# Building the gate one-hots of a PEER layer token by token, with keys in a row, in place of four wide comparisons and products a batch

## The reference

```
v1, i1 = top_k(s1, 16);  v2, i2 = top_k(s2, 16)            # per token and head (8 heads)
vals, ci = top_k(v1[:, None] + v2[None, :], 16)
e = i1[ci // 16] * 128 + i2[ci % 16]                       # 128 picks a token
g = softmax(vals)
a = gelu(x . u_tab[e])
out = sum_k g[k] * a[k] * v_tab[e[k]]
```

## Time and profile before

| what | us |
|---|---|
| three runs | 2448.03, 2458.07, 2462.87 (median 2458.07) |
| profiled execution | 2466.9 |
| its span | 2465.1 |
| TensorE busy | 2270.6 (92%) |
| VectorE busy | 1850.8 (75%) |
| ScalarE busy | 1188.8 (48%) |
| GpSimd busy | 422.4 (17%) |

### The profile page before, as it was taken

One profiled execution on the slowest core, in us unless ns is written; L12 is line 12 of the kernel. 1 busy time (PEld: TensorE's weight loads), 2 busy tenths in 40 slices (PEclk: granted clock), 3 DMA queues, 4 the chain that ended last, 5 costly groups with the idle time before them and its releaser, 6 DMA issues. The chain is left out here.

```text
span 2465.1 us, 33782 instructions
## 1 busy us (share of the span) xinstructions
PE 2270.6 (92%) x11984; PEld 1244.1 (50%) x11984; DVE 1850.8 (75%) x4125; ACT 1188.8 (48%) x1631; POOL 422.4 (17%) x395
## 2 busy tenths in 40 slices
PE   6799998897787998989999999998999999999997
PEld 3466665443454673435555555554444444444443
DVE  2566544554677655788979797994599999999999
ACT  1565463325566834542222223555665555555553
POOL 0011110000010210021212122442022222222220
PEclk9899999898898998999999999999999999999999
DMA  9565562000754944457787878899688887777781
GB/s 386 215 210 176 183 212 73 9 24 3 282 183 154 340 165 155 158 197 243 249 291 252 306 246 298 296 334 398 233 308 298 312 295 292 292 293 297 290 302 68
DMA packets 192077, 574.31 MB, mean 233 GB/s; under 512 B 18465, under 2 KB 52033, under 8 KB 184257
## 3 DMA queue, kind: packets, MB, share of 16 engines
q1 hardware_dynamic: 113872, 329.69, 38.8%
q0 software_dynamic: 47104, 167.80, 18.5%
q10 hardware_dynamic: 30960, 75.07, 7.8%
HBM read 455.48 MB, written 117.00 MB: 232 GB/s over the span
## 5 line engine op out<-in xcount | busy, mean ns | idle before, releaser
L297 PE MATMUL u_ps<-h_hi,lin_hi 128*128 128x512 f16 x1024 | 399.3, 390 | 9.2 <-PEq L74 9.2
L297 PE MATMUL u_ps<-h_lo,lin_hi 128*128 128x512 f16 x1024 | 398.2, 389 | 0.0
L297 PE MATMUL u_ps<-h_hi,lin_lo 128*128 128x512 f16 x1024 | 397.7, 388 | 0.0
L279 DVE SCALAR_TENSOR_TENSOR lin_lo<-lin_raw,lin_wsc,lin_hi 128x1024 f16<-128x1024 f32 x132 | 169.1, 1283 | 162.6 <-ACT lin_hi L273 162.3
L2346 PE MATMUL ps_w<-oh_buf 128*128 128x128 f16 x1024 | 281.3, 275 | 1.1 <-ACT region L2056 1.0
L1949 POOL DMA_INDIRECT row<-u_rows_dram,picked x128 | 168.8, 1319 | 651.1 <-DVE dot_junk L2127 466.4
L1886 POOL DMA_INDIRECT row<-v_dram,picked x128 | 177.4, 1386 | 536.0 <-DVE acc L2475 450.3
L273 ACT ACTIVATE lin_hi<-lin_raw,lin_wsc 128x1024 f16<-128x1024 f32 x132 | 151.1, 1146 | 191.0 <-DVE lin_wsc L138 141.4
L2586 PE MATMUL y_ps<-region 128*128 128x512 f16 x512 | 194.7, 380 | 1.4 <-PEq L1890 1.4
L2588 PE MATMUL y_ps<-region 128*128 128x512 f16 x512 | 194.7, 380 | 0.0
L2587 PE MATMUL y_ps<-region 128*128 128x512 f16 x512 | 194.6, 380 | 0.0
(11 more groups left out here) (398 smaller groups left out, 4416.1 us busy)
## 6 DMA issues: line engine op xcount, KB each, us to landing
lin_raw<-w_all_dram SPq DMA_DIRECT2D x132, 512.0 KB, 6.0
act_scratch<-activated ACTq DMA_DIRECT2D x128, 256.0 KB, 4.4
wgt_scratch<-region ACTq DMA_DIRECT2D x64, 512.0 KB, 6.1
region<-v_dram SPq DMA_DIRECT2D x15, 2048.0 KB, 7.5
oh_buf<-v_dram SPq DMA_DIRECT2D x15, 2048.0 KB, 7.5
proj<-w_mod_dram SPq DMA_DIRECT2D x16, 1536.0 KB, 12.0
act_buf<-w_all_dram SPq DMA_DIRECT2D x38, 512.0 KB, 4.3
lin_hi<-split_scratch SPq DMA_DIRECT2D x64, 256.0 KB, 3.3
```

The costliest lines, as they stand in the source:

```text
L279: nc.vector.scalar_tensor_tensor(out=self.lo[b][:], in0=self.raw[b][:], scalar=self.wsc[:, self.col(b)], in1=self.hi[b][:], op0=ALU.mult, ...
L297: last = nc.tensor.matmul(self.ps[b % 2][:, half, 0:ts.stop - ts.start], w_[:, kc, :], x_[:, kc, ts], start=(j == 0 and kc == 0), stop=(j ...
```

## The change

A batch's one-hots are now built by 24 instructions, one for each of 8 tokens and three outputs, each on 128 keys that lie next to each other. The one-input comparison takes the key table `iota_h` (128 f16 numbers) and a pointer operand with one value per partition, the pick of this token; for the second one-hot a second pointer operand, the gate, is multiplied in the same instruction, once with the high and once with the low part. The picks and gates are held in f32 for this, so that the high gate is first rounded to f16 (`gate_hi`) and then copied. The slots are laid out with the keys innermost, and the gate matmuls read both operands without a step. The wide table `iota_x`, its load and its conversion go. One semaphore, counted up by the last of the 24, stands for the four of before.

```diff
@@
-            pick_t = sb(c5, "pick_t", [P, 4, P], F16)
+            pick_t = sb(c5, "pick_t", [P, 4, P])
+            gate_hi = sb(c5, "gate_hi", [P, P], F16)
             iota_r = sb(c5, "iota_r", [P, NK])
-            iota_x = sb(c5, "iota_x", [P, NK, QB], F16)
-            slots = [second.onehots[:, n, :].rearrange("p (g k n) -> p g k n", g=2, k=NK) for n in range(9)]
+            iota_h = sb(c5, "iota_h", [P, NK], F16)
+            slots = [second.onehots[:, n, :].rearrange("p (g n k) -> p g n k", g=2, k=NK) for n in range(9)]
@@
                 sp.dma_start(iota_r[:], a["iota_r"]).then_inc(s("ld_iota"), 16)
-                sp.dma_start(iota_f, a["iota_x"]).then_inc(s("ld_iota"), 16)
@@
-                dve.wait_ge(s("ld_iota"), 32)
-                V.tensor_copy(iota_x[:, :, :].rearrange("p k n -> p (k n)"), iota_f).then_inc(s("iota"), 1)
+                dve.wait_ge(s("ld_iota"), 16)
+                V.tensor_copy(iota_h[:], iota_r[:]).then_inc(s("iota"), 1)
@@
-                    V.tensor_scalar(pick_t[:, 2, :], ps_p[:, 2, :], GATE_UP, None, ALU.mult).then_inc(s("pick_t"), 1)
-                    dve.wait_ge(s("pick_t"), 3 * t + 2)
-                    V.scalar_tensor_tensor(out=pick_t[:, 3, :], in0=ps_p[:, 2, :], scalar=GATE_UP, in1=pick_t[:, 2, :],
+                    V.tensor_scalar(gate_hi[:], ps_p[:, 2, :], GATE_UP, None, ALU.mult).then_inc(s("pick_t"), 1)
+                    dve.wait_ge(s("pick_t"), 4 * t + 2)
+                    V.tensor_copy(pick_t[:, 2, :], gate_hi[:]).then_inc(s("pick_t"), 1)
+                    V.scalar_tensor_tensor(out=pick_t[:, 3, :], in0=ps_p[:, 2, :], scalar=GATE_UP, in1=gate_hi[:],
                                            op0=ALU.mult, op1=ALU.subtract).then_inc(s("pick_t"), 1)
-                    dve.wait_ge(s("pick_t"), 3 * t + 3)
+                    dve.wait_ge(s("pick_t"), 4 * t + 4)
@@ def onehots(t, k):
-                    every = iota_x[:, :, :].unsqueeze(1).to_broadcast([P, 2, NK, QB])
-                    b, cs = k % 3, slice(k * OB, k * OB + OB)
-
-                    def spread(n):
-                        return pick_t[:, n, cs].rearrange("p (g n) -> p g n", g=2).unsqueeze(2).to_broadcast([P, 2, NK, QB])
+                    b = k % 3
                     dve.wait_ge(s("gates_mm1"), NBATCH * t + max(k - 2, 0))
-                    V.tensor_tensor(o2[b][1][:], every, spread(1), ALU.is_equal).then_inc(s("oh2"), 1)
-                    V.tensor_tensor(o1[b][:], every, spread(0), ALU.is_equal).then_inc(s("oh1"), 1)
-                    dve.wait_ge(s("oh2"), NBATCH * t + k + 1)
-                    V.tensor_tensor(o2[b][0][:], o2[b][1][:], spread(2), ALU.mult).then_inc(s("onehot_hi"), 1)
-                    dve.wait_ge(s("onehot_hi"), NBATCH * t + k + 1)
-                    V.tensor_tensor(o2[b][1][:], o2[b][1][:], spread(3), ALU.mult).then_inc(s("onehot"), 1)
+                    for g, out in ((1, o2[b][0]), (2, o2[b][1]), (0, o1[b])):
+                        for i in range(OB):
+                            tok = k * OB + i
+                            dst = out[:, i // QB, i % QB, :]
+                            if g:
+                                ins = V.tensor_scalar(dst, iota_h[:], pick_t[:, 1, tok:tok + 1], pick_t[:, g + 1, tok:tok + 1],
+                                                      ALU.is_equal, ALU.mult)
+                            else:
+                                ins = V.tensor_scalar(dst, iota_h[:], pick_t[:, 0, tok:tok + 1], None, ALU.is_equal)
+                    ins.then_inc(s("onehot"), 1)
@@ def gates(t, k):
                     pe.wait_ge(s("onehot"), NBATCH * t + k + 1)
-                    pe.wait_ge(s("oh1"), NBATCH * t + k + 1)
...
-                                ins = nc.tensor.matmul(ps_w[half][:, j, :], o1[b][:, half, :, j], o2[b][g][:, half, :, j],
+                                ins = nc.tensor.matmul(ps_w[half][:, j, :], o1[b][:, half, j, :], o2[b][g][:, half, j, :],
                                                        start=(g == 0), stop=(g == 1))
```

More of the change, by code:

```diff
@@ L1935, in build @@
             ROUTE_OPS = 16 * 5 + PH * 7
-            iota_f = eq[:, :, :].rearrange("p a j -> p (a j)").bitcast(F32)[:, 0:NK * QB]
             def at(t, m):
@@ L2688, in constants @@
         "iota_r": np.tile(np.arange(NK, dtype=f), (P, 1)),
-        "iota_x": np.tile(np.repeat(np.arange(NK, dtype=f), OB // 2), (P, 1)),
     }
```

## The result

The changed kernel takes **2568.88 us** (median, 2564.97 to 2572.01) against 2455.49 us (2448.03 to 2462.87) for the kernel before in the same rounds: ratio 1.046, 95% interval 1.0431 to 1.0490, or 113 us slower. The forecast was 2572 us, +114. The profiled execution of the changed kernel took 2565.0 us (span 2563.2).

A forecast was written before the change was run, and what follows sets the result against it. TensorE was taken to pace the first two periods, VectorE close behind; slower one-hots make VectorE the pace. Period terms of +27.2, +27.7, +29.9, +31.6 and -2 sum to +114 on 2458: 2572 us, range 2545 to 2640.

The forecast's parts named there:

- The batch: VectorE's one-hots: 8 one-pointer instructions at 0.164 us plus 16 two-pointer at 0.224, 4.9 us against 2.53.
- The periods: Four tile stretches of the third stage: +27.2, +27.7, +29.9, +31.6 us, and -2 behind the last one-hots.
- The waits that were to vanish: VectorE's waits on the exponential (22.2 us in two tiles), TensorE's total (8.5) and gathered rows (6.8) go.
- the gain: Gate matmuls on TensorE, keys in a row: 0.06 us each instead of 0.117, up to 1.0 us less a batch.
- TensorE's idle time: TensorE stands still 2 to 3 us in each column, after its eighth matmul, waiting for the one-hots.
- The small things: Wide index table's load gone: -0.4 us, taken as 0; second semaphore costs nothing; gather delay taken as 0.
- Rival C: Last tile's gathers each held up 4.9 us, so gathered rows run out: +80, 2652 us; chance 0.05.
- One sign of the prediction: Before 1140 us and after the last one-hots nothing should change length by more than 3 us.
- the other form of rival B: By the skill's fixed 75 ns per VectorE instruction, a batch takes 2.6 us, ending within 2 us of 2427.
- A (width brings nothing): VectorE's f16 one-hot instructions run at the f32 rate: +0.8 us a batch, +51, 2623 us; chance 0.22.
- B (small instructions are cheap): VectorE's pointers hidden, batch 2.5 us, and TensorE gets its gain: -31, 2427 us; chance 0.08.
- D, the clock: TensorE's clock falls from standing still: 3 to 4 us per slow column, some 15 in all; no own chance.

The follow-up runs named there:

- the f32 table: Changed kernel with the key table read in f32 (iota_r) instead of f16, all else the same: 2627.25 us, ratio 1.0685.
- constants: Changed kernel with constants in place of the pointer operands of the 24 one-hot instructions: 2418.38 us, ratio 0.9852.
- step reads: Changed kernel with gate matmuls reading the slots with a step of 4 elements as before: 2567.0 us, ratio 1.0458.
- row reads: Kernel before, four large one-hot instructions kept, gate matmuls reading 128 elements in a row: 2431.56 us, ratio 0.9881.
- pairs innermost: Kernel before, four large instructions kept, slots with 2 tokens innermost instead of 4, so matmuls read every second element: 2426.36 us, ratio 0.9866.

## Why the prediction was right

**The batch.** Forecast 0.164 and 0.224 us start to start, 4.9 us together; measured 0.163, 0.223 and 4.87. Both halves of the estimate held: the fixed part taken from f32 rows with pointers (the kernel with the f32 table repeats them within 0.002 us), and the 33 ns for the width (32 and 36 measured). The kernel with constants shows that 0.060 us of this fixed part is each pointer's, as taken. What is left without pointers is 0.102 us, of it 0.069 fixed. The Trainium skill, Vector Engine (DVE) Microarchitecture Reference, section on measured stream behaviour on trn2, gives about 75 ns fixed; with the 33 ns of streaming that is an estimate of 0.108 us, and the trace comes within 6 ns of it. The section names no cost of pointer operands, and for those the rows of the kernel before were the better source.

**The periods.** Forecast +27.2, +27.7, +29.9, +31.6 and -2; measured +26.0, +26.7, +28.1, +31.1 and -3.4 (the end of the last tile's dot products to the end of the span). The first three are 1.0 to 1.8 us under: 16 batches cost 37.4 us more and not 38.4. The worked terms gave 2.37 us a batch, I had rounded that up to 2.4, and 2.34 was measured. The third has a second part: I had let VectorE's shorter waits on ScalarE's high part stand (line 279), and the longer of them shrank from 3.1 to 1.3 us. The waits that were to vanish did, to the last one, and nothing took their place, since ScalarE's exponential was ready before VectorE asked for it.

**TensorE.** 219 ns in a row (the median; 236 is the mean with matmuls at the lower clock) and 0.055 us each, against 0.06 taken. The kernel with step reads shows the gain hidden; the one with row reads shows what of it the time keeps until VectorE's own work stops it. TensorE's idle time is 27 us in each of the first two tiles, 1.7 us a column, less than the 2 to 3 forecast, because the lower clock filled part of it (12.7 us a tile, last section).

**The small things.** The table's load was taken as 0; the means with and without it are 1.4 us apart. The gathers were not held up: GpSimd's group in the changed kernel

```profile
L1949 POOL DMA_INDIRECT row<-u_rows_dram,picked x128 | 155.8, 1217 | 772.8 <-DVE dot_junk L2126 589.9
```

has a mean of 1217 ns where it was 1319, and no dot product waits for a row. Rival C did not occur.

**How exact it is.** The median rose by 113 us, the span of the profiled executions by 98: 111.8 in the periods, -2.4 from the stage's first instructions to the first one-hots, -3.4 at the end, and -8.0 ahead of the stage, where both kernels do the same. In twelve profiled kernels that stage began anywhere from 920.3 to 932.4 us. Without those 8.0 the parts add up to +106, and the interval of the ratio is +106 to +120. So the match of the medians within 1 us of +114 is partly luck; the periods are the fair test. One sign of the prediction did not hold: nothing before the first one-hots or behind the last was to change by more than 3 us, and the one became 10.4 us shorter, most of it the scatter just named, the other 3.4. Small slips in the working change nothing: the third period lacks the 0.15 us of the added copy, and the other form of rival B, a batch of 2.6 us, would end some 4 us above its 2427, not within 2.

**The rivals.** A (width brings nothing) is refuted by the f32 table, 52 us slower in the four tiles and 58 by the medians. B (small instructions are cheap) is what happens without pointers: 2418 us, forecast for it 2427. D, the clock, did fall to 0.90, and cost nothing that the sum needed: with step reads it was 0.96, and the period the same to 0.03 us. Where it was low, a column lost 2.6 us (last section), under the 3 to 4 taken as the most.

## What to carry to other kernels

Count pointer operands, not only instructions: here each added 60 ns to a VectorE instruction of 0.10 us, so one large instruction with a broadcast operand (0.60 us for 1024 elements) beats eight small ones with pointers, though they do two operations at once. A layout need not be all one consumer's: with pairs innermost the writer kept its four large instructions and the reader got its full speed. And before giving one engine's time to another, read who has slack in that stage: VectorE had 0.7 us a batch, the change asked for 2.3.

## What the runs showed of the hardware that was not expected

**A step of four f16 elements in the moving operand** makes a 128-column matmul 275 ns instead of 220 and its start-to-start cost 0.117 instead of 0.057 us; a step of two costs nothing. The Trainium skill, SBUF — State Buffer, section on the DMA port swizzle, has lines of 16 bytes that want two hits each and calls steps up to 8 bf16 free. Four f16 elements are 8 bytes, two hits a line. The trace of TensorE's gate matmuls disagrees: that step was not free (275 ns), one of 4 bytes was (220).

**The clock is low after a wait within a column.** TensorE's timeline in the changed kernel after a standstill of 3.37 us:

```profile
1152.12 0.29 PE L2345 MATMUL ps_w<-oh_buf 128*128 128x128 f16 x1 [3.37 <-DVE oh_buf L2263]
1152.20 0.63 PE L297 MATMUL u_ps<-h_hi,lin_hi 128*128 128x512 f16 x1
...
1157.00 0.63 PE L297 MATMUL u_ps<-h_hi,lin_hi 128*128 128x512 f16 x1
...
1161.05 0.38 PE L297 MATMUL u_ps<-h_hi,lin_hi 128*128 128x512 f16 x1
...
1163.76 0.38 PE L297 MATMUL u_ps<-h_lo,lin_hi 128*128 128x512 f16 x1
```

Nine pairs in 4.80 us are 0.533 us each, ten later ones in 2.71 us are 0.271. The granted clock is 0.50 from 1152.20 to 1157.50 us and 1.00 from 1157.90 on: the lower level of 1.2 GHz, then 2.4 GHz. Ten such pairs lose some 2.6 us in that column. In a first period TensorE is busy for 132.95 us at a clock of 0.90, where the kernel with pairs does the same 741 matmuls in 120.27 at 1.00: its idle time cost it 12.7 us a tile, most of the 15 us (256 x 0.06) that the quicker reads had given, and the time shows none of it, since VectorE set the pace. With step reads it stood still less, and the clock was 0.96.
